# Moving the softmax scaling of two attention blocks from VectorE to ScalarE

## What is computed

```
logits = where(allowed, logits, -inf)
p = softmax(logits, axis=-1)            # exp(x - max) / sum
o = einsum('bthk,btkc->bthc', p, v)
```

## Time and profile before

| what | value |
|---|---|
| time, median of 3 runs | 878.95 us (877.04 to 881.04) |
| the profiled execution: its time, its span | 883.51 us, 881.7 us |
| busy share of the span: PE, DVE, ACT, POOL | 87%, 45%, 39%, 46% |
| mean granted TensorE clock | 0.948 of full speed |
| layer 1 attention loop | about 129 to 260 us of the span |
| layer 2 attention loop | about 455 to 526 us |

### The profile page before, as it was taken

The page is one execution under the profiler, slowest core; times in us unless marked ns, Lnnn a source line. Parts: engine busy times, 40 slices in busy tenths (PEclk is TensorE's granted clock), DMA queues, the critical chain, the costliest instruction groups (busy, mean ns, idle before and its releaser), DMA issues.

```text
span 881.7 us, 14663 instructions
## 1 busy us (share of the span) xinstructions
PE 771.3 (87%) x5552; PEld 629.8 (71%) x5552; DVE 393.6 (45%) x702; ACT 344.0 (39%) x618; POOL 407.0 (46%) x320
## 2 busy tenths in 40 slices
PE   3889998889989996999879999965998888888885
PEld 2879988788979985998769989944554444444455
DVE  3538943469891234207736664265122222222224
ACT  4434468565643345454256654332121111111122
POOL 2446846576868973786966658520010000000000
PEclk9888999899999998999899999997899999999989
DMA  9413423233434542353334334751679999999921
GB/s 362 158 48 109 179 97 143 97 119 122 145 141 147 188 148 91 144 175 131 128 140 144 109 132 148 282 239 49 270 290 422 422 422 422 422 422 422 422 111 48
DMA packets 25972, 181.01 MB, mean 205 GB/s; under 512 B 3008, under 2 KB 3264, under 8 KB 4416
## 3 DMA queue, kind: packets, MB, share of 16 engines
q1 hardware_dynamic: 25920, 180.29, 52.9%
HBM read 179.23 MB, written 1.05 MB: 204 GB/s over the span
## 4 chain that ended last, share of the span: by engine, by line
PE 60%; DMA 17%; DVE 13%; ACT 6%; issue 3%; SPq 1%; POOL 0%; POOLq 0%; DVEq 0%; ACTq 0%
PE D L481 38%; DMA ring<-w_expert_dram 16%; PE D L835 6%; PE UB L522 2%; PE L L593 2%; DVE big_r L1344 2%; ACT ring_r L961 1%; PE D L812 1%; DVE hT L1327 1%; PE QB L481 1%; PE TB L602 1%; DVE big_r L1349 1%; PE QB L856 1%; PE L L856 1%; DVE attn L1447 1%
## 5 line engine op out<-in xcount | busy, mean ns | idle before, releaser
L1277 POOL TENSOR_TENSOR ring_r<-ring,ring_r 128x512 fp32r<-128x512 f32 x280 | 382.4, 1393 | 185.5 <-ACT ring_r L961 185.0
L481 PE MATMUL D<-scr_r,ring_r 128*128 128x256 f32 x1344 | 263.3, 293 | 2.4 <-POOL ring_r L1277 1.5
L481 PEld LDWEIGHTS D<-scr_r,ring_r 128*128 128x128 f32 x1344 | 218.9, 197 | 5.4 <-issue 3.8
L961 ACT ACTIVATE ring_r<-ring 128x1024 fp32r<-128x1024 f32 x140 | 146.7, 1056 | 176.8 <-PE D L481 159.6
L481 PE MATMUL D<-hT_r,ring_r 128*128 128x256 f32 x672 | 193.2, 288 | 0.0
L835 PE MATMUL D<-ring,small 128*64 128x256 f32 x960 | 117.7, 390 | 27.3 <-DMA ring<-w_expert_dram 21.0
L481 PE MATMUL D<-big_r,ring_r 128*128 128x256 f32 x1038 | 130.0, 288 | 5.8 <-DVE big L1592 5.2
L481 PEld LDWEIGHTS D<-big_r,ring_r 128*128 128x128 f32 x1038 | 128.8, 197 | 6.6 <-DVE big L1592 5.6
L481 PEld LDWEIGHTS D<-hT_r,ring_r 128*128 128x128 f32 x672 | 132.5, 197 | 1.2 <-issue 1.0
L835 PEld LDWEIGHTS D<-ring,small 128*64 128x64 f32 x960 | 68.7, 139 | 87.1 <-DMA ring<-w_expert_dram 37.0
L1291 POOL COPY small<-big 128x512 f32 x31 | 19.4, 627 | 215.3 <-PE D L835 196.7
(11 more groups left out here) (291 smaller groups left out, 911.0 us busy)
## 6 DMA issues: line engine op xcount, KB each, us to landing
ring<-w_expert_dram SPq DMA_DIRECT2D x90, 1024.0 KB, 11.5
ring<-w_dense_dram SPq DMA_DIRECT2D x70, 1024.0 KB, 4.8
big<-w_expert_dram SPq DMA_DIRECT2D x2, 1024.0 KB, 7.9
cst<-consts_dram SPq DMA_DIRECT2D x1, 1408.0 KB, 10.3
xT<-x_t_dram SPq DMA_DIRECT2D x2, 512.0 KB, 4.6
big<-w_rg_dram SPq DMA_DIRECT2D x1, 1024.0 KB, 18.1
wu<-w_expert_dram SPq DMA_DIRECT2D x1, 1024.0 KB, 6.9
attn<-w_expert_dram SPq DMA_DIRECT2D x1, 1024.0 KB, 8.9
```

The costliest lines, as they stand in the source:

```text
L481: last = mm(out_, r32(w[i][ws]), r32(x[j][xs_]), start=start and m == 0, stop=stop and m == 2)
L961: A_(r32(hi_unit(j)), dense_unit(j), ACT.Copy).then_inc(hi_ready, 1)
L1277: last = g.tensor_tensor(r32(w), w, r32(h).bitcast(F32), ALU.subtract)
```

## The change

ScalarE multiplies E by the inverse sums; VectorE only inverts them. A new semaphore `summed` goes from VectorE's reciprocal to ScalarE, and `probs` is now raised by ScalarE. In layer 1 the multiplication stands behind `side_gate` of the same head, in layer 2 right behind `exps`.

```
             # scalar engine
+            def normalise(a):
+                act.wait_ge(summed, a + 1)
+                for tt in range(NT):
+                    c0, n = (0, P) if tt == 0 else (P, T)
+                    last = A_(E[:, a % 2, c0:c0 + n], E[:, a % 2, c0:c0 + n], ACT.Copy,
+                              scale=stat[:, a % 2, 2, tt:tt + 1])
+                last.then_inc(probs, 1)
...
                     if m < H1 // 2:
                         exps(2 * m + j)
                         side_gate(2 * m + j)
+                        normalise(2 * m + j)
                         if m < 2:
                             decays(4 * m + 2 * j, 4 * m + 2 * j + 2)
...
                     if m < H2:
                         exps(H1 + 2 * m + j)
+                        normalise(H1 + 2 * m + j)
...
             # vector engine
             def normalise(a):
                 dve.wait_ge(expd, a + 1)
-                step(v.reciprocal(stat[:, a % 2, 2, :], stat[:, a % 2, 1, :]))
-                for tt, (c0, n) in enumerate(tiles):
-                    last = v.tensor_scalar(E[:, a % 2, c0:c0 + n], E[:, a % 2, c0:c0 + n],
-                                           stat[:, a % 2, 2, tt:tt + 1], None, ALU.mult)
-                last.then_inc(probs, 1)
+                v.reciprocal(stat[:, a % 2, 2, :], stat[:, a % 2, 1, :]).then_inc(summed, 1)
```

More of the change, by code:

```diff
@@ L285, in build @@
         v1_mm, v1_ready = sem("values_matmul"), sem("values_ready")
-        logits, biased, maxed, expd, probs = [sem(n) for n in ("logits", "biased", "maxed", "expd", "probs")]
+        logits, biased, maxed, expd, summed, probs = [sem(n) for n in (
+            "logits", "biased", "maxed", "expd", "sum_inverted", "probs")]
         pt_mm, pt_ready, o_mm, o_ready = [sem(n) for n in ("probs_transposed", "pt_ready", "o_matmul", "o_ready")]
```

## The result

The changed kernel takes 889.36 us (median of 4, 888.03 to 892.54) where the kernel before took 878.00 (875.62 to 881.04). The ratio is 1.0131, with a 95% interval of 1.0101 to 1.0161: 11 us slower. A second series of six executions gave 889.02 us and 1.0130 (1.0096 to 1.0163). The forecast was 885.2 us in a range of 879.5 to 891, slower at 64%: the side was right, and so was the mechanism of the waits; the loss came out at 11 us instead of 6.

What follows compares the result with a forecast made beforehand. TensorE was taken as the bound, with ScalarE's list on the path early in layer 1's loop. Layer 1 +3.8, layer 2 +0.9 and clock +1.5 give +6.2 us on 879.0: 885.2 us, range 879.5 to 891.

Steps and rivals of the forecast that it cites:

- the mechanism of the waits: Layer 1: ScalarE's pairs delay keys_in and ptcopy, so TensorE's waits grow by about 0.7 us per pair ahead.
- The price of a pair: ScalarE's two scaled copies per head: 0.71 us, taken from exponentials of the same shapes; between 0.55 and 1.2.
- The -0.19: Layer 1, pass 5: VectorE's 2.55 us pair is gone, exponentials come earlier, TensorE's 0.19 us wait disappears.
- The 0.15 for `keys_in` in passes 4 to 6: Layer 1: keys_in there has just enough slack for a pair; three passes at about 0.05 us each.
- The sum, +3.8: Layer 1's terms: 0.9 + 1.42 + 0.71 + 0.71 - 0.19 + 0.15 + 0.12 us.
- VectorE's relief: Layer 1, passes 4 to 7: about 12 us leave VectorE's list, but are hidden behind TensorE.
- a forecast of 0.9: Layer 2's last pass: pairs and reciprocal waits delay the ptcopy TensorE's transposes need; +0.9 us (0.6 to 1.2).
- one slow stretch more: Layer 1: of two lengthened TensorE waits, one brings another stretch of half-speed matmuls, +1.5 us.
- No slow stretch is added: Rival, 25%: everything as forecast without the clock term, +4.7 us, 883.7 us.
- hidden anyway: Rival, 15%: ScalarE's extra work in passes 0 to 2 fits or is given back; +0 to +2, 880 us.
- VectorE the bound: Rival, 7%: VectorE bounds layer 1's passes 4 to 7, so the change gains up to 4.4 us, about 874.6.
- ScalarE layer 2's bound: Rival, 8%: pairs over 1.28 us make ScalarE bound layer 2's loop; at 1.5 us a pair, about 893 us.

Runs made afterwards that it cites:

- the useless matmuls: TensorE makes matmuls nobody reads in layer 1's waits: added to the changed kernel 887.74 us, added to the kernel before 881.22 us.
- the run without multiplication: Multiplication by the inverse sums left out on both engines, VectorE still inverting; total not compared, layer 1's loop 129.7 us (130.7 before).
- the moved order: Changed kernel with ScalarE's layer 1 pairs moved behind keys_in or ptcopy: 880.40 us; same with layer 2 given back to VectorE: 876.14 us.
- layer 1 alone: Against the changed kernel, ScalarE multiplies only in layer 1, VectorE again in layer 2: 885.19 us, ratio 1.0060.
- layer 2 alone changed: VectorE multiplies in layer 1, ScalarE in layer 2: 881.88 us; same with 12 useless matmuls before the last head's transposes: 880.67 us.
- the doubled pair: Changed kernel with each of ScalarE's pairs followed by a second pair of plain copies in place: 902.09 us, ratio 1.0278.

## Why the prediction was right, and where it was too small

**The price of a pair.** Taken from the exponentials as 0.71 us; measured 0.69 from start to start. Right.

**Layer 1, wait by wait.** Forecast +0.9 in pass 0, +1.42 in pass 1, +0.71 in pass 2, +0.71 in pass 4. The waits grew by 0.78, 0.70 + 0.69, 0.69 and 0.66 us. The -0.19 came as said. For pass 4 the forecast was too high all the same: with the useless matmuls in both kernels that wait grew by 0.29 us only, and in the two other profiles by 0.14 and 0.18 against the 1.55 of before. The 0.15 for `keys_in` in passes 4 to 6 did not come; instead there are 0.25 us in pass 3 in two of the four profiles. At the end the last transposes' wait grew by 0.68 us, and VectorE's split no longer came last, as said; but the matmuls behind that wait ran at half speed, and the next projection started 2.58 us behind the transposes, as late as before (2.56), where 1.90 was possible. The sum, +3.8, stands against 3.3 us of waiting at full clock.

**VectorE's relief is hidden.** Shown by the run without multiplication and by the moved order, both with loop 1 no shorter than other kernels with the waits of before have it. VectorE was 17 us less busy in the second half of loop 1, where about 10 was forecast.

**Layer 2.** Covered but for the last pass. The exponentials of the last pass started 0.2 us sooner, counted from the loop's first scores, and the wait grew by 0.97 us for a forecast of 0.9. Loop 2 grew by 1.2; the other 0.2 us is the last products of the loop, already at half speed. The wait for the reciprocal was 0.23 us and 0.27 was taken.

**The clock, the step that was mis-sized.** The prediction took one slow stretch more, at 1.5 us, and looked at loop 1 alone. The price of a stretch was about right and their number was not. Loop 1 took 138.0, 136.8 and 136.9 us in the three profiles with the changed order (the changed kernel twice and layer 1 alone), mean 137.2. With the waits of before it took 130.7, 128.8 and 127.1 (before, and the two with layer 2 alone changed), mean 128.9. Of these 8.3 us, 3.3 are waiting, so the clock costs loop 1 about 5.0 us more, for 1.5 forecast, from few profiles: 2.3 more slow stretches on average instead of one, and one at the loop's end, 0.7 to 0.9 us. By these loops and their full-clock lengths a stretch inside cost 1.7 to 1.9 us. The prediction priced no slow stretch at the end of either loop. Behind loop 2 the way to the router's first matmul took 57.9 us instead of 56.7. The account: 3.3 + 1.0 of waiting, 5.0 + 0.2 + 1.3 of clock, 10.8 us for a measured 11.4. It leaves out the part between the two loops, which was 0.8 to 1.0 us longer in the same three profiles than before; other kernels had 192.9 to 196.4 us there, and what makes that is not shown. The waiting terms are tied to their cause by the moved order and the doubled pair, the clock in loop 1 by the useless matmuls and by where the slow stretches lie. Which wait brings one in a given execution is not settled, and the split of the clock's part is rough to a microsecond or two.

**What was luck.** That 889.4 us lies inside the range owes something to chance. The forecast's own mechanism gave 885 to 887 us; the upper end of 891 was set from the rival in which ScalarE bounds layer 2's loop, and that did not happen.

**The rivals.** "No slow stretch is added" is refuted by the clocks; "hidden anyway" by the waits; "VectorE the bound" by the run without the multiplication and the two with the moved order; "ScalarE layer 2's bound" by loop 2, in which TensorE waited only at the end even with the pair doubled.

## What to carry to other kernels

Moving work to the less busy engine is priced by what stands behind its new place in that engine's list. With layer 1's 16 pairs in front of two hand-offs that TensorE waited for, the kernel lost 11 us; with the same pairs some lines further down it lost 1 us, which cannot be told from none. Where a wait of the busiest engine ends at an in-order engine, read what that engine did just before the hand-off; here most of it could go behind, which was worth 8 us. A longer wait of TensorE costs more than its length when it is followed by matmuls at half speed, so each should be priced with that.

## What the runs showed of the hardware

In the kernel before, unchanged, the time goes with the mean granted clock: of 77 executions, the 28 at 0.956 or 0.958 took 875.6 to 877.2 us and the 12 at 0.948 took 882.6 to 883.4. It is not one line (four at 0.949 took 878.5 to 878.9). From 0.956 to 0.948 is 2 x 0.008 x 880, by estimate 14 us more at the 1.2 GHz level, for 7 us of time.

The length of a wait alone did not say whether the clock fell. Behind the wait of 2.94 us the scores of pass 3 took 0.93 us, full speed, in one profile and 1.23 and 1.65 in two others; before, behind 2.25, they took 1.65. Behind 3.35 us the scores of pass 2 took 1.66 us in the kernel before and 0.93 in the one with layer 2 alone changed. Behind 2.06 us they took 0.93, with half speed from 143 us on, and 1.65 and 1.66 in the two others. What the profiles do show is the number: 0 to 2 slow stretches in loop 1 with the waits of before, 3 or 4 with the longer ones. Useless matmuls of TensorE in the waits kept loop 1 at 0.99 to 1.00 in both kernels, but did not make a faster kernel.
